# Filling all four weight slots behind each projection of the first mixer, with its convolutions as steps of their own

## The chip, the core and the metric

The kernel runs on one core of a Trainium2 chip. The metric is the device time of one execution in microseconds (us), where less is better. TensorE is called PE in the profile, VectorE DVE, ScalarE ACT, GpSimd POOL and SyncE SP (its DMA queue SPq).

## The reference

Two blocks of two layers each run over one sequence of 256 tokens with a width of 1024, all in float32. The change is mostly about the mixer of the first block:

```python
h = rms_norm(x, norm1_g)
proj = h @ w_in
qkv = silu(causal_depthwise_conv(qkv, dn_conv_w))      # four taps
q, k = l2_normalize(q), l2_normalize(k)
beta, g = sigmoid(b_in), -exp(dn_a_log) * softplus(a_in + dn_dt_bias)
o_dn = chunk_gated_delta_rule(q, k, v, g, beta)        # needs the inverse of a unit triangular matrix
o_dn = rms(o_dn) * dn_norm_g * silu(z)
y = gate_b * causal_depthwise_conv(gate_c * hv, sc_conv_w)   # three taps
x = x + concatenate([o_dn, rms(y)]) @ w_out
x = x + (silu(h2 @ ffn_w_gate) * (h2 @ ffn_w_up)) @ ffn_w_down
```

The second block takes its norms' scale and shift from `mod = silu(c) @ mod_w[l] + mod_b[l]`. This is a product of one row with a matrix of 1024 x 9216 per layer. It doesn't depend on `x`, so the kernel works it out beside the feed-forward stages (FFN).

## The kernel before

**Products in three parts.** Every float32 weight is split into a rounded high part and the rest: `h @ w` is `h_hi w_hi + h_lo w_hi + h_hi w_lo`. The weights come as units of 128 x 1024. ACT writes the high part of a unit (`round_weights`, the instruction on L970) and DVE the low part (`low_weights`, L1282, which waits for ACT's). PE may start a unit once its low part is there (`s_lo_ready`). `w_hi` and `w_lo` have four slots each, so unit v can be rounded once unit v - 4 has been used.

**Loads.** Two units make a chunk of 1 MB. SP loads chunks in the order of the steps into `raw`, a ring of four (L466). The load of chunk c waits until chunk c - 4 is used up: until the low parts of both its units are made, or, where it is a "mod" chunk, until DVE has reduced it. Most mod chunks go into a ring of their own (`side`, six places, L457). Those numbered 40 to 47 go through `raw`, since the memory of `side` is in use then.

**One list of steps.** `FIRST` and `SECOND` write out the order of a layer's steps by hand, and each engine walks through the same list and does its share of each step. An engine runs its instructions strictly in this order: what stands first and waits holds up all behind it. At a step with products, ACT and DVE first see to it that the weights are made up to two units past the step's own (`round_weights(n["split"] + units + 2)`, and `low_weights` with the same limit); at a filler step (mod, coef, table) up to four units from the next one on.

**The first mixer.** Its projections are pairs of 128-column tiles. `lead` is the first product of a pair and `pair` the second, each of 24 matmuls. For pairs 0 to 5 (q, k, v) ACT scales and copies both tiles out of PSUM (L1104, L1106) and DVE then adds three taps of the convolution in six instructions (L1440), both at the step `pair`. `silu` is a tanh on ACT (L1109) and a product on DVE (L1448). Pairs 6 and 7 are z (a tanh on ACT, L1112, and a product on DVE, L1454), pairs 8 to 11 are the short convolution (a copy on ACT, L1114, then L1460 to L1468 on DVE). `nsum` squares a tensor on ACT (L979) and sums it on PE (L714): 1 for k, 0 for q. `decay` is a chain through PE, DVE (L1426 to L1429) and ACT (L1084 to L1094). `kk` and `kq` are the products of keys and queries. `lvt` and `lvx` (1 to 6) build the triangular inverse level by level, each on PE (L763 and L774), then ACT (L1147) or DVE (L1552, L1555; level 6 on L1570). `scan` (L819 and what follows) is the recurrence. Both layers have this mixer, with the same times relative to its start.

**The FFN.** 33 steps: four `gu` (two wide products each, gate and up), then down, gu, gu in turn (`ffn_order`). Steps 4, 7, 10, ... are `down`. After a `gu`, ACT copies its sums to `sq` (L1186), DVE adds the rest (L1589), ACT takes a tanh (L1006), DVE makes `hid` (L1312, L1313), ACT rounds it (L1000), and POOL makes its low part (L1807), which `down` needs. `behind_ffn` spreads a list of mod steps over an FFN, here 20, 22 and 26 of them over the FFNs of block 1 layer 0, block 1 layer 1, and the second one of block 2 layer 0. `behind_steps` with `RAW_MODS` puts the eight raw mods behind steps 2, 6, 10, ..., 30 of the first FFN of block 2 layer 0. Each mod is two reductions on DVE (L1401). `COEFS` are small operations for the second mixer, put behind the steps in `COEF_STEPS`.

Of the kernel before, what the change touches and what calls it, by code (L numbers as in the profile page):

```python
# [48 lines left out]
COEFS = [("coef", 0), ("coef", 1), ("coef", 2), ("coef", 3), ("coef", 4), ("table", 0), ("coef", 5), ("table", 1),  # L49
         ("coef", 6), ("kzero", 0), ("coef", 7), ("table", 2), ("coef", 8), ("table", 3), ("coef", 9), ("table", 4),  # L50
         ("bzero", 0), ("table", 5), ("table", 6), ("table", 7)]
RAW_MODS = {2 + 4 * k: k for k in range(8)}
COEF_STEPS = [k for k in range(3, 29) if k not in RAW_MODS]
BLK = T // 2


def ffn_order():

    out = [("gu", k) for k in range(4)]
    for j in range(FT // 2):  # L60
# [4 lines left out]


FIRST = (
    [("norm", 0), ("pair", 0), ("crow", 0), ("lead", 1), ("silu", 0), ("pair", 1), ("gates", 0), ("lead", 6),
     ("silu", 1), ("pair", 6), ("gsum", 0), ("lead", 2), ("pair", 2), ("lead", 3), ("decay", 0), ("silu", 2),
     ("pair", 3), ("lead", 8), ("silu", 3), ("pair", 8), ("lead", 9), ("nsum", 1), ("nroot", 1), ("pair", 9), ("kk", 0),  # L70
     ("kq", 0), ("lead", 4), ("pair", 4), ("lead", 5), ("silu", 4), ("lvt", 1), ("tokk", 0), ("pair", 5), ("lvx", 1),
     ("lead", 10), ("silu", 5), ("lvt", 2), ("nsum", 0), ("nroot", 0), ("lvx", 2),
     ("pair", 10), ("lvt", 3), ("lead", 11), ("lvx", 3), ("pair", 11), ("lead", 12), ("lvt", 4),
     ("pair", 12), ("lvx", 4), ("lead", 13), ("lvt", 5), ("pair", 13), ("lvx", 5), ("tokv", 0), ("lead", 7),
     ("nsum", 2), ("lvt", 6), ("nroot", 2), ("pair", 7), ("lvx", 6), ("nrow", 2), ("scan", 0),
     ("out", 0), ("nsum", 3), ("nroot", 3), ("out", 1), ("nrow", 3), ("out", 2), ("dsplit", 0)]
# [23 lines left out]
    + [s for k, step in enumerate(ffn_order()) for s in  # L100
       [step] + [("grow", 0)] * (k == 9) + [c for at, c in zip(COEF_STEPS, COEFS) if at == k]]
    + [("post", 0), ("pre", 1)] + MIXER
# [6 lines left out]
FFN_STEPS = len(ffn_order())  # L109


def behind_ffn(steps, which, mods):

    places = [k for k, s in enumerate(steps) if s[2] in ("gu", "down")][which * FFN_STEPS + 6:(which + 1) * FFN_STEPS - 4]
    out, done = [], 0
    for k, s in enumerate(steps):
        out.append(s)
        if k in places:
            upto = len(mods) * (places.index(k) + 1) // len(places)
            out += mods[done:upto]  # L120
            done = upto
    return out
# [17 lines left out]
def second_block(L):  # L140
    return [(2, L, kind, i) for kind, i in SECOND]
# [4 lines left out]
        [(1, LAYERS - 1, "final", 0)] + \  # L146
        behind_ffn(behind_steps(second_block(0), 0, MODS[1][4:12], RAW_MODS), 1, MODS[1][12:]) + second_block(1)
SIDE_OF = {m: k for k, m in enumerate([m for m in range(MODT) if not 40 <= m < 48])}
# [36 lines left out]
AT = {(B, L, kind, i): n for B, L, kind, i, n in NUMBERED}  # L185
# [20 lines left out]
def build(nc, w, x_in, const_in, p1_in, p2_in, bt_in, out):  # L206
    with ExitStack() as ctx:
# [31 lines left out]
        crow = sb("crow", [P, D])  # L239
# [189 lines left out]
        def evacuated(e, *step):  # L429

            p = AT[step]["pair"]
            e.wait_ge(banks[p % 2], p // 2 + 1)
# [518 lines left out]
        def _(act):  # L951
# [64 lines left out]
            for B, L, kind, i, n in NUMBERED:  # L1016
                bank = stream[n["pair"] % 2]
                units = units_of(B, kind, i)
# [76 lines left out]
                elif kind == "pair" and B == 1 and i < 6:  # L1095
# [6 lines left out]
                    for e in range(2):  # L1102
                        last_tap = (2 * i + e) * TAPS + TAPS - 1
                        f(yv[:, 2 * (i % 2) + e, :], bank[:, e, :], ACT.Copy,  # L1104
                          scale=p1_(L, "conv", last_tap, last_tap + 1))
                    f(rawp[:, i % 2, :, 3:3 + T], bank[:], ACT.Copy).then_inc(free, 1)  # L1106
                elif kind == "silu":
                    act.wait_ge(s_conv_done, 12 * L + 2 * (i + 1))
                    f(th[:, 2 * (i % 2):2 * (i % 2) + 2, :], yv[:, 2 * (i % 2):2 * (i % 2) + 2, :], ACT.Tanh,  # L1109
                      scale=0.5).then_inc(s_th_done, 1)  # L1110
                elif kind == "pair" and B == 1 and i < 8:
                    f(zs[:, 2 * (i - 6):2 * (i - 6) + 2, :], bank[:], ACT.Tanh, scale=0.5).then_inc(s_z_th, 1)  # L1112
                elif kind == "pair" and B == 1 and i < 12:
                    f(sc[:, i - 8, :], bank[:, 0, :], ACT.Copy).then_inc(s_c_done, 1)  # L1114
                elif kind == "nsum":
                    src = [qT, kT, sc, None][i]

                    def n_ready(j):
# [121 lines left out]
                elif kind == "score":  # L1240
# [3 lines left out]
                    for e, cols in enumerate((slice(0, T), slice(T, T + P))):  # L1244
                        k = 2 * i + e
# [20 lines left out]
        def _(dve):  # L1266
# [3 lines left out]
            def link(ins):  # L1270
                links[0] += 1
                ins.then_inc(s_dve_self, 1)
                dve.wait_ge(s_dve_self, links[0])
# [3 lines left out]
            def low_weights(limit):  # L1277

                while fed[0] < min(limit, TOTAL["split"]):
                    q = fed[0]  # L1280
                    dve.wait_ge(s_hi_ready, q + 1)
                    v.tensor_tensor(w_lo[:, q % SLOTS, :],  # L1282
                                    raw[:, chunk_of_unit[q] % RAWS, (q % 2) * UNIT:(q % 2 + 1) * UNIT],
                                    w_hi[:, q % SLOTS, :].bitcast(F32), ALU.subtract).then_inc(s_lo_ready, 1)
                    fed[0] += 1
# [38 lines left out]
            for B, L, kind, i, n in NUMBERED:  # L1324
                bank = stream[n["pair"] % 2]
                units = units_of(B, kind, i)
# [63 lines left out]
                elif kind == "mod":  # L1390
                    dve.wait_ge(s_crow_done, 2)
                    if n["mod"] in SIDE_OF:
                        k = SIDE_OF[n["mod"]]
# [30 lines left out]
                elif kind == "decay":  # L1424
# [2 lines left out]
                    dve.wait_ge(s_gc_sb, L + 1)  # L1427
                    v.tensor_tensor(sm["d"], sm["gc"][:, 8:16], sm["gc"][:, 0:8], ALU.subtract).then_inc(s_dd_done, 1)
                    v.tensor_scalar(sm["ngc"], sm["gc"][:, 0:8], -1.0, None, ALU.mult).then_inc(s_dd_done, 1)  # L1429
                elif kind == "pair" and B == 1 and i < 6:  # L1430
                    evacuated(dve, B, L, kind, i)
                    if L == 0 and i == 0:
                        dve.wait_ge(s_pads, 1)
                    for k in range(TAPS - 1):
                        for e in range(2):
                            tile = 2 * i + e
                            y = yv[:, 2 * (i % 2) + e, :]
                            src = rawp[:, i % 2, e, k:k + T]
                            tap = p1_(L, "conv", tile * TAPS + k, tile * TAPS + k + 1)
                            ins = v.scalar_tensor_tensor(y, src, tap, y, ALU.mult, ALU.add)  # L1440
                            if k == TAPS - 2:
                                ins.then_inc(s_conv_done, 1)
                            elif e == 1:
                                link(ins)
                elif kind == "silu":
                    dve.wait_ge(s_th_done, 6 * L + i + 1)
                    dst = (qT, kT, vT)[i // 2]
                    v.scalar_tensor_tensor(dst[:, 2 * (i % 2):2 * (i % 2) + 2, :], th[:, 2 * (i % 2):2 * (i % 2) + 2, :],  # L1448
                                           1.0, yv[:, 2 * (i % 2):2 * (i % 2) + 2, :], ALU.add, ALU.mult)\
                        .then_inc(s_silu_done, 1)  # L1450
                elif kind == "pair" and B == 1 and i < 8:
                    t = 2 * (i - 6)
                    dve.wait_ge(s_z_th, 2 * L + i - 5)
                    v.scalar_tensor_tensor(zs[:, t:t + 2, :], zs[:, t:t + 2, :], 1.0, bank[:], ALU.add, ALU.mult)\  # L1454
                        .then_inc(free, 1)
                elif kind == "pair" and B == 1 and i < 12:
                    t = i - 8
                    dve.wait_ge(s_c_done, 4 * L + t + 1)
                    dve.wait_ge(s_pads, L + 1)
# [2 lines left out]
                    for k in range(STAPS):  # L1462
# [3 lines left out]
                            link(v.tensor_scalar(sc[:, t, :], src, tap, None, ALU.mult))  # L1466
                        else:
                            link(v.scalar_tensor_tensor(sc[:, t, :], src, tap, sc[:, t, :], ALU.mult, ALU.add))  # L1468
                elif kind == "pair" and B == 1:
                    t = 2 * (i - 12)  # L1470
                    v.tensor_tensor(sc[:, t:t + 2, :], sc[:, t:t + 2, :], bank[:], ALU.mult).then_inc(free, 1)
                elif kind == "nsum" and i == 3:
# [221 lines left out]
                elif kind == "fwd":  # L1694
                    k = 4 * L + i
# [10 lines left out]
                elif kind == "rec":  # L1706
                    k = 4 * L + i
# [7 lines left out]
                elif kind == "back":  # L1715
                    k = 4 * L + i
# [259 lines left out]
```

## Time and profile before

| | |
|---|---|
| Median of 3 runs | 1954.5 us (1952.48 to 1957.59) |
| Time of the profiled execution | 1957.57 us |
| Its span | 1955.2 us |
| PE busy | 1849.3 us, 95% of the span |
| DVE busy | 1472.1 us, 75% |
| ACT busy | 1064.5 us, 54% |
| POOL busy | 202.4 us, 10% |
| DMA engines busy (mean share, three queues) | 52.8% |
| TensorE clock granted, mean | 0.976 of full speed |

Times in the timeline count from the start of the span. By the timeline the first mixer of layer 0 lies at about 21 to 183 us and that of layer 1 at 381 to 540 us. The FFN with raw mods lies at 743 to 942 us, and the one with 26 mod steps at 1154 to 1347 us.

### The profile page before, as it was taken

The numbers are of one execution on the slowest core, as the hardware profiler recorded it, in microseconds if no ns is written. First come the engines' busy times: TensorE is split into PE (matmuls) and PEld (weight loads), VectorE is DVE, ScalarE is ACT, GpSimd is POOL, SyncE is SP. The second block draws the span as 40 slices with busy tenths as digits, with TensorE's granted clock in tenths as the row PEclk, the third lists the DMA queues.
The fourth block names the chain that finished last, engine by engine and source line by source line (L and its number), as shares of the span: only waits on it lengthen the run. The fifth ranks groups of instructions, "written<-read, shape, count | busy, mean of one in ns | idle before, by whom it ended". The sixth has DMA issues, their size and how long they took to land.

```text
span 1955.2 us, 31506 instructions
## 1 busy us (share of the span) xinstructions
PE 1849.3 (95%) x12640; PEld 1627.5 (83%) x12640; DVE 1472.1 (75%) x2339; ACT 1064.5 (54%) x1739; POOL 202.4 (10%) x174
## 2 busy tenths in 40 slices
PE   6999999998999998999799989998999899989998
PEld 5887888788978887888699978877888799978887
DVE  4756799875578987888677768997777767776565
ACT  5645555664465456656534565446566744556554
POOL 0100111101011111111000001110111100001111
PEclk9989999998999999999899989998999999999999
DMA  5332898433369864555343449974545343344452
GB/s 219 121 111 107 324 346 331 156 135 110 111 264 357 319 220 162 215 216 215 131 150 130 158 179 359 362 301 160 194 173 193 130 152 122 119 170 167 178 194 86
DMA packets 53280, 383.50 MB, mean 196 GB/s; under 512 B 5904, under 2 KB 6032, under 8 KB 6928
## 3 DMA queue, kind: packets, MB, share of 16 engines
q1 hardware_dynamic: 53136, 381.50, 52.4%
q8 instruction: 100, 1.64, 0.3%
q14 instruction: 44, 0.36, 0.1%
HBM read 380.43 MB, written 1.05 MB: 195 GB/s over the span
## 4 chain that ended last, share of the span: by engine, by line
PE 74%; DVE 13%; ACT 7%; issue 4%; DMA 2%; POOL 0%; SPq 0%; DVEq 0%; ACTq 0%
PE quad L505 20%; PE quad L506 10%; PE quad L495 6%; PE quad L496 5%; PE quad L497 5%; PE works L517 4%; PE works L519 4%; PE works L518 4%; ACT w_hi L970 3%; DVE w_lo L1282 3%; DMA raw<-w 2%; DVE mx L1401 2%; DVE mx L1440 1%; PE works L676 1%; PE works L888 1%
## 5 line engine op out<-in xcount | busy, mean ns | idle before, releaser
L1282 DVE TENSOR_TENSOR w_lo<-raw,w_hi 128x1024 fp32r<-128x1024 f32 x572 | 700.5, 1233 | 211.5 <-ACT w_hi L970 209.9
L505 PE MATMUL quad<-h_two,w_hi 128*128 128x512 f32 x2112 | 755.9, 401 | 14.5 <-DVE h_two L1290 9.7
L970 ACT ACTIVATE w_hi<-raw 128x1024 fp32r<-128x1024 f32 x572 | 595.8, 1054 | 213.6 <-PE quad L506 95.2
L506 PE MATMUL quad<-h_two,w_lo 128*128 128x256 f32 x2112 | 596.2, 282 | 0.0
L505 PEld LDWEIGHTS quad<-h_two,w_hi 128*128 128x128 f32 x2112 | 401.1, 190 | 116.5 <-issue 18.7
L506 PEld LDWEIGHTS quad<-h_two,w_lo 128*128 128x128 f32 x2112 | 403.1, 191 | 2.0
L1807 POOL TENSOR_TENSOR g_lo<-hid,g_hi 128x256 fp32r<-128x256 f32 x140 | 177.5, 1269 | 1516.4 <-ACT g_hi L1000 1516.4
L495 PE MATMUL quad<-h_two,w_hi 128*128 128x256 f32 x960 | 280.3, 292 | 10.7 <-DVE w_lo L1282 10.7
L496 PE MATMUL quad<-h_two,w_hi 128*128 128x256 f32 x960 | 274.2, 286 | 0.0
L497 PE MATMUL quad<-h_two,w_lo 128*128 128x256 f32 x960 | 273.7, 285 | 0.0
L495 PEld LDWEIGHTS quad<-h_two,w_hi 128*128 128x128 f32 x960 | 186.3, 194 | 15.6 <-issue 13.9
L517 PE MATMUL works<-w_hi,g_hi 128*128 128x512 f32 x480 | 189.2, 394 | 0.4 <-DVE w_lo L1282 0.4
L519 PE MATMUL works<-w_lo,g_hi 128*128 128x512 f32 x480 | 187.7, 391 | 0.0
L518 PE MATMUL works<-w_hi,g_lo 128*128 128x512 f32 x480 | 187.2, 390 | 0.0
L496 PEld LDWEIGHTS quad<-h_two,w_hi 128*128 128x128 f32 x960 | 186.6, 194 | 0.0
L497 PEld LDWEIGHTS quad<-h_two,w_lo 128*128 128x128 f32 x960 | 186.4, 194 | 0.0
L1401 DVE CUSTOM_DVE_ANT_0 mx<-mx,crow 128x1024 f32<-128x1024 f32 x128 | 151.0, 1217 | 0.0
L1000 ACT ACTIVATE g_hi<-hid 128x256 fp32r<-128x256 f32 x140 | 57.4, 412 | 149.3 <-DVE hid L1313 145.6
L1186 ACT ACTIVATE sq<-quad 128x512 f32<-128x512 f32 x132 | 78.0, 591 | 99.8 <-PE quad L506 99.3
L1589 DVE TENSOR_TENSOR sq<-sq,quad 128x512 f32<-128x512 f32 x132 | 90.2, 683 | 53.8 <-ACT sq L1186 53.2
L519 PEld LDWEIGHTS works<-w_lo,g_hi 128*128 128x128 f32 x480 | 90.1, 188 | 20.3
L517 PEld LDWEIGHTS works<-w_hi,g_hi 128*128 128x128 f32 x480 | 90.1, 188 | 19.9 <-issue 0.7
(408 smaller groups left out, 2184.2 us busy)
## 6 DMA issues: line engine op xcount, KB each, us to landing
raw<-w SPq DMA_DIRECT2D x294, 1024.0 KB, 4.9
mx<-w SPq DMA_DIRECT2D x64, 1024.0 KB, 7.0
par<-p_in SPq DMA_DIRECT2D x2, 1110.0 KB, 7.1
x<-x_in SPq DMA_DIRECT2D x1, 1024.0 KB, 5.6
mx<-bt_in SPq DMA_DIRECT2D x2, 512.0 KB, 6.0
out<-x SPq DMA_DIRECT2D x4, 256.0 KB, 2.3
con<-const_in SPq DMA_DIRECT2D x1, 428.0 KB, 3.0
par<-p_in SPq DMA_DIRECT2D x1, 225.0 KB, 5.7
```

Source lines behind the costliest of these rows:

```text
L495: mm(o, hi, r_hi[:, kt, :], start=first, stop=False, skip_group_check=True)
L496: mm(o, hi, r_lo[:, kt, :], start=False, stop=False, skip_group_check=True)
L497: last = mm(o, lo, r_hi[:, kt, :], start=False, stop=end, skip_group_check=True)
L505: mm(o, hi, h_two[:, kt, :, :], start=kt == 0, stop=False, skip_group_check=True)
L506: return mm(o[:, 0:T], lo, h_hi[:, kt, :], start=False, stop=kt == DT - 1, skip_group_check=True)
L517: mm(sums[q][:], a_hi, hi, start=first, stop=False)
L518: mm(sums[q][:], a_lo, hi, start=False, stop=False)
L519: last = mm(sums[q][:], a_hi, lo, start=False, stop=end)
L970: f(w_hi[:, v % SLOTS, :], raw[:, chunk_of_unit[v] % RAWS, (v % 2) * UNIT:(v % 2 + 1) * UNIT], ACT.Copy).then_inc(s_hi_ready, 1)
L1282: v.tensor_tensor(w_lo[:, q % SLOTS, :], raw[:, chunk_of_unit[q] % RAWS, (q % 2) * UNIT:(q % 2 + 1) * UNIT], w_hi[:, q % SLOTS, :].bitcast ...
L1401: v.tensor_tensor_reduce(rows, rows, crow[:], 1.0, 0.0, ALU.mult, ALU.add, modacc[:, 2 * i + e:2 * i + e + 1]).then_inc(s_mod_used, 1)
L1807: v.tensor_tensor(g_lo[:, slot, :], hid[:, g % 2, :], g_hi[:, slot, :].bitcast(F32), ALU.subtract)\
```

## The change

- `pair` 0 to 5 is split: ACT's copies stay at `pair`, and DVE's part becomes a step `conv`, placed by hand. At `conv` DVE waits for ACT's copies, does the six instructions, and then makes low parts up to four units past the pair's own. For pair 1 it stands behind `gates`, for 0, 2, 3 and 4 behind the next `lead`, and for 5 behind `lvx` 2.
- At the end of `pair` 0 to 11, ACT rounds weights up to four units past the pair's own; DVE does the same with the low parts at the end of `pair` 6 to 11.
- `nsq` 0, the squares of q on ACT, stands behind `kq`. PE's sum and `nroot` 0 stay where `nsum` 0 is.
- `silu` 5 moves from behind `lead` 10 to behind `pair` 10.
- The raw mods stand behind steps 2, 4, 6, 10, 14, 18, 22 and 26. `coef` 0 and 1 move from behind steps 3 and 4 to behind 1 and 3 (in both layers); the others stay.
- `behind_ffn` starts one step earlier, at 5, and spreads over 24 places in place of 23.

```diff
-RAW_MODS = {2 + 4 * k: k for k in range(8)}
-COEF_STEPS = [k for k in range(3, 29) if k not in RAW_MODS]
+RAW_MODS = {at: k for k, at in enumerate((2, 4, 6, 10, 14, 18, 22, 26))}
+COEF_STEPS = [1] + [k for k in range(3, 29) if k not in RAW_MODS]
 FIRST = (
-    [("norm", 0), ("pair", 0), ("crow", 0), ("lead", 1), ("silu", 0), ("pair", 1), ("gates", 0), ("lead", 6),
-     ("silu", 1), ("pair", 6), ("gsum", 0), ("lead", 2), ("pair", 2), ("lead", 3), ("decay", 0), ("silu", 2),
-     ("pair", 3), ("lead", 8), ("silu", 3), ("pair", 8), ("lead", 9), ("nsum", 1), ("nroot", 1), ("pair", 9), ("kk", 0),
-     ("kq", 0), ("lead", 4), ("pair", 4), ("lead", 5), ("silu", 4), ("lvt", 1), ("tokk", 0), ("pair", 5), ("lvx", 1),
-     ("lead", 10), ("silu", 5), ("lvt", 2), ("nsum", 0), ("nroot", 0), ("lvx", 2),
-     ("pair", 10), ("lvt", 3), ("lead", 11), ("lvx", 3), ("pair", 11), ("lead", 12), ("lvt", 4),
+    [("norm", 0), ("pair", 0), ("crow", 0), ("lead", 1), ("conv", 0), ("silu", 0), ("pair", 1), ("gates", 0),
+     ("conv", 1), ("lead", 6), ("silu", 1), ("pair", 6), ("gsum", 0), ("lead", 2), ("pair", 2), ("lead", 3), ("conv", 2),
+     ("decay", 0), ("silu", 2), ("pair", 3), ("lead", 8), ("conv", 3), ("silu", 3), ("pair", 8), ("lead", 9), ("nsum", 1),
+     ("nroot", 1), ("pair", 9), ("kk", 0), ("kq", 0), ("nsq", 0), ("lead", 4), ("pair", 4), ("lead", 5), ("conv", 4),
+     ("silu", 4), ("lvt", 1), ("tokk", 0), ("pair", 5), ("lvx", 1),
+     ("lead", 10), ("lvt", 2), ("nsum", 0), ("nroot", 0), ("lvx", 2), ("conv", 5),
+     ("pair", 10), ("silu", 5), ("lvt", 3), ("lead", 11), ("lvx", 3), ("pair", 11), ("lead", 12), ("lvt", 4),
      ("pair", 12), ("lvx", 4), ("lead", 13), ("lvt", 5), ("pair", 13), ("lvx", 5), ("tokv", 0), ("lead", 7),
      ("nsum", 2), ("lvt", 6), ("nroot", 2), ("pair", 7), ("lvx", 6), ("nrow", 2), ("scan", 0),
...
 def behind_ffn(steps, which, mods):
-    places = [...][which * FFN_STEPS + 6:(which + 1) * FFN_STEPS - 4]
+    places = [...][which * FFN_STEPS + 5:(which + 1) * FFN_STEPS - 4]
...
 ACT, kind == "pair" and B == 1 and i < 6:
                     f(rawp[:, i % 2, :, 3:3 + T], bank[:], ACT.Copy).then_inc(free, 1)
+                    round_weights(n["split"] + units + 4)
 ACT, kind == "pair" and B == 1 and i < 8 (and the same at i < 12):
                     f(zs[:, 2 * (i - 6):2 * (i - 6) + 2, :], bank[:], ACT.Tanh, scale=0.5).then_inc(s_z_th, 1)
+                    round_weights(n["split"] + units + 4)
 ACT:
-                elif kind == "nsum":
+                elif kind in ("nsum", "nsq") and (kind, i) != ("nsum", 0):
 DVE:
-                elif kind == "pair" and B == 1 and i < 6:
-                    evacuated(dve, B, L, kind, i)
+                elif kind == "conv":
+                    evacuated(dve, 1, L, "pair", i)
...
+                    low_weights(AT[1, L, "pair", i]["split"] + units_of(1, "pair", i) + 4)
 DVE, at the end of pair 6, 7 and of pair 8 to 11:
+                    low_weights(n["split"] + units + 4)
```

## Rows read from the trace of the kernel before

**Rows 1.** The page: each engine's busy time.

```profile
PE 1849.3 (95%) x12640; PEld 1627.5 (83%) x12640; DVE 1472.1 (75%) x2339; ACT 1064.5 (54%) x1739; POOL 202.4 (10%) x174
```

**Rows 2.** Busy time by stretch: us, PE, PEld, DVE, ACT, POOL, clock, DMA, GB/s.

```profile
380.00:457.00 77.00, 67.71 (x680) 65.66 (x680) 57.67 (x112) 50.22 (x96) 9.21 (x9) 1.00 0.33 116
461.00:469.00 8.00, 8.00 (x135) 7.82 (x136) 2.01 (x4) 0.22 (x1) 0.00 (x0) 0.56 0.26 86
740.00:941.00 201.00, 192.35 (x1060) 162.77 (x1059) 164.95 (x248) 122.19 (x179) 28.22 (x22) 0.98 0.53 214
```

**Rows 3.** Waits of PE, 380 to 540 us: total us, times, longest.

```profile
PE quad L495 <- DVE w_lo L1282: 5.4, 5, 1.3
PE works L763 <- DVE mx L1552: 3.1, 1, 3.1
```

**Rows 4.** Timeline of ACT at pair 3 (layer 1).

```profile
419.25 0.83 ACT L1104 ACTIVATE mx<-quad,par 128x256 f32<-128x256 f32 x2
...
420.45 1.07 ACT L970 ACTIVATE w_hi<-raw 128x1024 fp32r<-128x1024 f32 x1
...
426.12 1.14 ACT L979 ACTIVATE sq<-mx 128x512 f32<-128x512 f32 x2
```

**Rows 5.** Timeline of DVE at pair 3 (layer 1).

```profile
420.67 2.71 DVE L1440 SCALAR_TENSOR_TENSOR mx<-mx,par 128x256 f32<-128x256 f32 x6
423.31 1.22 DVE L1282 TENSOR_TENSOR w_lo<-raw,w_hi 128x1024 fp32r<-128x1024 f32 x1
```

**Rows 6.** Timeline of PE, 427 to 464 us.

```profile
427.61 1.84 PE L714 MATMUL quad<-con,sq 128*128 128x1 f32 x16
...
457.33 0.83 PE L763 MATMUL works<-mx 32*32 32x32 f32 x64 [3.10 <-DVE mx L1552]
459.24 3.54 PE L714 MATMUL quad<-con,sq 128*128 128x1 f32 x16 [1.08 <-ACT sq L979]
...
463.69 0.58 PE L495 MATMUL quad<-h_two,w_hi 128*128 128x256 f32 x1
```

**Rows 7.** Timeline of DVE, then of PE, ahead of the scan (layer 1).

```profile
503.62 0.69 DVE L1454 SCALAR_TENSOR_TENSOR mx<-mx,quad 128x512 f32<-128x512 f32 x1 [1.19 <-ACT mx L1112]
504.23 0.74 DVE L1570 TENSOR_SCALAR mx<-works 64x256 f32<-64x256 f32 x2
...
505.77 1.06 PE L819 MATMUL works<-mx 128*128 128x128 f32 x8
```

**Rows 8.** Loads of raw, 745 to 800 us: all issues on L466.

```profile
DMA to landing us min/median/max: 4.8/6.9/10.3
```

**Rows 9.** Timelines of ACT, DVE and PE, 762 to 783 us.

```profile
770.22 1.06 ACT L970 ACTIVATE w_hi<-raw 128x1024 fp32r<-128x1024 f32 x1 [1.80 <-DMA raw<-w]
...
765.25 0.08 DVE L1401 DVE_READ_ACCUMULATOR2_ANT modacc<- 128x1 f32 x1
...
771.19 0.39 PE L505 MATMUL quad<-h_two,w_hi 128*128 128x512 f32 x1
```

**Rows 10.** DVE and PE at the end of the FFN, layer 0, then layer 1.

```profile
928.74 1.22 DVE L1401 CUSTOM_DVE_ANT_0 raw<-raw,crow 128x1024 f32<-128x1024 f32 x1
...
931.03 0.42 DVE L1312 SCALAR_TENSOR_TENSOR gate_t<-gate_t,sq 128x256 f32<-128x256 f32 x1
...
933.68 0.80 PE L535 MATMUL works<-w_hi,g_hi 128*128 128x512 f32 x1 [4.99 <-POOL g_lo L1807]
...
1542.50 0.50 PE L535 MATMUL works<-w_hi,g_hi 128*128 128x512 f32 x1 [0.34 <-POOL g_lo L1807]
```

**Rows 11.** DVE, then PE, behind step 21 of the FFN with 26 mods.

```profile
1287.44 1.22 DVE L1401 CUSTOM_DVE_ANT_0 mx<-mx,crow 128x1024 f32<-128x1024 f32 x1
...
1292.03 0.42 DVE L1312 SCALAR_TENSOR_TENSOR gate_t<-gate_t,sq 128x256 f32<-128x256 f32 x1
...
1294.19 0.77 PE L505 MATMUL quad<-h_two,w_hi 128*128 128x512 f32 x1 [2.64 <-DVE w_lo L1282]
1294.96 0.63 PE L505 MATMUL quad<-h_two,w_hi 128*128 128x512 f32 x1
```

More of the change, by code:

```diff
@@ L112, in behind_ffn @@
 def behind_ffn(steps, which, mods):
-    places = [k for k, s in enumerate(steps) if s[2] in ("gu", "down")][which * FFN_STEPS + 6:(which + 1) * FFN_STEPS - 4]
+    places = [k for k, s in enumerate(steps) if s[2] in ("gu", "down")][which * FFN_STEPS + 5:(which + 1) * FFN_STEPS - 4]
     out, done = [], 0
@@ L1112, in _ @@
                     f(zs[:, 2 * (i - 6):2 * (i - 6) + 2, :], bank[:], ACT.Tanh, scale=0.5).then_inc(s_z_th, 1)
+                    round_weights(n["split"] + units + 4)
                 elif kind == "pair" and B == 1 and i < 12:
                     f(sc[:, i - 8, :], bank[:, 0, :], ACT.Copy).then_inc(s_c_done, 1)
-                elif kind == "nsum":
+                    round_weights(n["split"] + units + 4)
+                elif kind in ("nsum", "nsq") and (kind, i) != ("nsum", 0):
                     src = [qT, kT, sc, None][i]
@@ L1450, in _ @@
                         .then_inc(s_silu_done, 1)
-                elif kind == "pair" and B == 1 and i < 8:
+                elif kind == "pair" and B == 1 and 6 <= i < 8:
                     t = 2 * (i - 6)
@@ L1455, in _ @@
                         .then_inc(free, 1)
-                elif kind == "pair" and B == 1 and i < 12:
+                    low_weights(n["split"] + units + 4)
+                elif kind == "pair" and B == 1 and 8 <= i < 12:
                     t = i - 8
@@ L1468, in _ @@
                             link(v.scalar_tensor_tensor(sc[:, t, :], src, tap, sc[:, t, :], ALU.mult, ALU.add))
-                elif kind == "pair" and B == 1:
+                    low_weights(n["split"] + units + 4)
+                elif kind == "pair" and B == 1 and i >= 12:
                     t = 2 * (i - 12)
```

## The prediction

> **What bounds the kernel.** I read the busy table first: PE is busy 95% of the span [rows 1], so only PE's pauses, and stretches at a lower clock, can be won. The stretches by stage come second. In the first mixer's earlier half PE is busy 67.7 of 77 us at full clock, while no other engine is full and DMA stands at 0.33; in the FFN with the raw mods it misses about 9 of 201 us [rows 2]. Third come PE's waits in the mixer: five waits for low parts of weights, 5.4 us; 3.1 us of `lvt` 2 for `lvx` 1's update on DVE [rows 3]; 1.08 us of `nsum` 0 for the squares of q shows in the timeline [rows 6]. Last, the timelines around each pause show what the late instruction stood behind. Both layers have the same mixer, so each figure for it counts twice.
>
> **Mixer, what is removed.** The five waits are worth 5.4 us [rows 3]. `lvx` 1 no longer stands behind convolution 5, and the squares of q are made early: the 3.10 and 1.08 us in front of `lvt` 2 and `nsum` 0 go [rows 6]. With them goes a stretch at the lower clock: the stretch from 461 us has a mean of 0.56 [rows 2], so between 1.2 and 2.4 GHz. PE was idle most of the 5 us before. It costs `nsum` 3.54 against 1.84 us elsewhere, 1.7 us [rows 6], and I put the product behind it at 2.0 us (its 24 matmuls of about 0.12 us each start over 24 x 0.12 = 2.9 us at full clock). In all 5.4 + 4.2 + 3.7 = 13.3 us per mixer.
>
> **Mixer, what is added.** The fill adds no instruction; it moves roundings ahead of other work on two engines that run in order. Four places matter.
>
> (a) At `lead` 3, 8 and 5 DVE's low part now stands ahead of the convolution, and waits for ACT's high part, which waits for ACT's copies. Before, convolution 3 started 1.42 us behind the start of the copies [rows 4, 5]. Now it is copies 1.33, rounding 1.0, low part 1.14: 3.5 us behind. ACT reaches the copies of pair 3 no earlier than before, since the chain of `decay` on ACT ends there: convolution 2, late by the same mechanism, starts `decay` some 0.9 us later, and one rounding of 0.95 us that stood behind it is gone. So the low part for `lead` 9 comes at about 422.8 (before 423.31 + 1.22 = 424.5), and PE waits there 3.3 us instead of 0.8, having been earlier by then.
>
> (b) Convolution 3 ends 2.1 us later, and the two roundings filled behind `pair` 8 (now 2.0 us, of which one stood there before) precede the squares of k. These start at 428.4 in place of 426.12 [rows 4], so `nsum` 1 starts at 429.1 in place of 427.61 [rows 6], after a second pause of about 3.2 us. PE is then 1.5 us later than before; the fifth wait's 1.2 us comes back behind it. The five weight waits are thus spent on two larger ones: net +0.2 us.
>
> (c) ACT's copies for `lvt` 1 and `lvt` 2 stand behind convolution 4's tanh and behind two filled roundings: `lvx` 1 and 2 wait 1.0 and 1.3 us. Net of the 13.3 us, PE reaches product `pair` 10 at about 459.6 in place of 463.69 [rows 6], and gains 2.0 more in it: 6.1 us.
>
> (d) Behind `pair` 7, DVE now makes two low parts (2.4 us) ahead of L1570, on which the scan waits. In the trace L1570 runs at 504.23 to 504.97, right behind L1454, and PE starts the scan at 505.77 with no pause [rows 7]. Now it ends at 507.5: +2.0 us. The scan's chain has no slack to return it.
>
> Without clock effects this is 6.1 - 2.0 = 4.1 us per mixer. But two pauses of over 3 us within 10 us of each other, with `nsum` behind the second, look like those that cost the clock at 461 us. A pause of only 2.64 us was enough in an FFN: its next matmuls are 0.63 us apart, against 0.35 later [rows 11]. I charge one slow stretch, `nsum` 1.7 and most of a product 1.6: 3.3 us. Ends: none, or twice that (a second one at `lvx` 2). Two mixers give -2 x (4.1 - 3.3) = **-1.6 us**.
>
> The Trainium skill, "TensorE: Matmul & The Clock Gate", section "Why this matters for your kernels", says that a long idle gap between bursts of matmuls sets the clock back; the 2.64 us row is shorter than the gap that it warns of, so the trace is harsher than the rule. If (a) and (b) were harmless as the rule would have it, the mixers would give -8.2 us.
>
> **FFN with raw mods, its end.** The mod behind step 30 goes. Its 2.3 us stand straight ahead of L1312, and through `hid`, ACT and POOL ahead of the last `down`, where PE waits 4.99 us; layer 1, without mods, waits 0.34 [rows 10]. I take 2.3 us; what is left is about 2.7 us of pause. The first matmul behind it takes 0.80 us instead of 0.50 [rows 10]: PE is at the lower clock there. If 2.7 us spares the clock, 2.5 us more.
>
> **FFN with raw mods, its start.** A mod behind step 4 takes a place in the ring of four. Chunk order becomes mod 0, gu 3, down 0, mod 1, gu 4. So gu 4's load, before the fourth behind nothing but gu 2, now waits until mod 0 is reduced, at 765.3 [rows 9]. A load takes 4.8 us at the least [rows 8] (gu 5's, which stood there before, landed in time for the rounding at 770.22 [rows 9]). Rounding 1.05 and low part 1.2 put gu 4 at 772.65 in place of 771.19 [rows 9]: +1.5. Worse, ACT and DVE stand still for it from 763 on. Behind it come, in order, the sum of gu 3 (773.2), a low part, coef 1, `hid` (775.9), two low parts (778.6), and only then mod 1, until 781.0. Down 1's load waits for that: landed at 785.8, low part ready at 788.1. PE is done with gu 5 at 772.65 + 4 x 2.83 = 784.0, and pauses 4.3 us. Together 5.8 us. The clock falls in it as it does at 933.68, so that charge moves rather than goes (2.5 us on both sides). Later mods stand where they stood, about 3 us more behind PE, which the 12 us between mod and need still covers. 5.8 - 2.3 = **+3.5 us**. Ends: -4.8 (the loads are in time) and +10 (down 2's load, which waits for mod 2, is late too).
>
> **The FFN with 26 mod steps.** By the formula, before there were two mods behind steps 13 and 21; now one more stands at 5 and the double is at 16. Both lists are at 9 behind step 13, 18 behind 21, and 24 behind 27. From step 13 on DVE has no free time (in the timeline its pauses are 0.2 to 0.3 us), and behind step 21 its 4.6 us of reductions make PE wait 2.64 us [rows 11]. Up to step 12 the new list has done 8 against 7, in DVE's free time: one reduction, 2.37 us, leaves the full stretch. **-2.4 us**; ends 0 and -4.2 (pause and slow matmuls both).
>
> **No cost.** The FFNs with 20 and 22 mods show no pause of PE over 0.34 us, and get no double: 0. The coef operations moved by a step are 12 of 0.2 us beside a full PE: 0.
>
> **Sum.** -1.6 + 3.5 - 2.4 = -0.5 us on the profiled span of 1955.2, the same on its own time of 1957.57; that execution is 3 us above the median, so I count from the median: 1954.5 - 0.5 = **1954.0 us**.
>
> **Rivals.**
> 1. The clock holds in the mixers, or the two new pauses are shorter than I count. For: they are split by a dense product. Against: the row of 2.64 us. -8.2 there, +3.5 - 2.5 = +1.0 and -2.4: -9.6, 1944.9. Chance 0.20.
> 2. Down 1's load comes in time, because DVE gets to mod 1 within 6 us rather than 15. The FFN gives -4.8 instead of +3.5: 1954.0 - 8.3 = 1945.7. Against: the ring's order leaves gu 4 no earlier load. Chance 0.10.
> 3. Slower: the raw ring stays late. Each mod is reduced late, the next load with it, and PE pauses at down 2 as at down 1: 4.3 and 2.5 of clock, +6.8: 1960.8. It decides if mod 2 ends later than 7 us ahead of down 2's start; I count 7.2 us, so it is near. Chance 0.23.
> 4. The fill does nothing: slots are free no earlier than the old order asked, and only `lvt` 2 gains and the scan pays. The time would still be 1952 to 1956. Chance 0.05.
>
> My forecast has 0.42. About 0.3% (5.9 us) is what a measurement of this kernel can tell from no change. Rivals 1 and 2 are faster by more (0.30), the forecast and rival 4 lie within (0.47), and rival 3 is slower (0.23). The range takes rivals 1 and 3 in: 1944 to 1963. The forecast alone, with its bounds, is 1949 to 1959.
>
> **What would show it.** PE's five waits for L1282 in the mixer gone; a pause of about 3 us ahead of `lead` 9 and one ahead of `nsum` 1, in both layers; `lvt` 2 without a pause; the scan starting behind L1570, with two low parts ahead of it. PE pausing about 4 us before down 1 of the FFN with raw mods, on DMA through ACT and DVE, and about 2.7 us at its end. No 2.64 us pause in the FFN with 26 mods. I am wrong if convolution 3 starts as early as before, or if down 1 starts without a pause.

## The result and the profile after

The changed kernel takes 1960.91 us (median of 15 runs, 1954.99 to 1965.86), against 1954.92 us (15 runs, 1949.06 to 1957.59) for the kernel before beside it: a ratio of 1.0029, 95% interval 1.0019 to 1.0038, so 5.7 us more (3.7 to 7.4). One further execution of the kernel before, beside e5 to e8, took 4619.77 us and, as the only slow one, is left out of every ratio. I had said 1954.0 us. The time lies inside my range, but it moved the way to which I gave 0.23. The profiled execution took 1963.98 us, its span is 1961.9 us.

Busy time of each engine, from the page of the changed kernel:

```profile
PE 1855.1 (95%) x12640; PEld 1631.8 (83%) x12640; DVE 1470.0 (75%) x2339; ACT 1065.7 (54%) x1739; POOL 199.7 (10%) x174
```

The counts are those of before [rows 1], and PE is busy 5.8 us longer with the same 12640 matmuls. The mean granted clock is 0.973, before 0.976, and 0.003 of 1960 us is 5.9 us. PE is idle for 106.8 us (the span less the busy time), before 105.9: of the 6.7 us between the two spans 0.9 us are pauses, and the rest is time at the lower clock.

Between the first transposition of one norm and that of the next, the timelines give this (us, before and after): mixer of layer 0 167.5 and 167.6, its FFN 193.7 and 193.6; mixer of layer 1 163.7 and 161.8, its FFN 197.1 and 201.1; FFN with raw mods 208.0 and 216.9; FFN with 26 mods 203.2 and 201.0. So one profile puts the loss into the raw FFN and into an FFN that the change touches only in the places of some of its mod steps, and shows the mixers no slower. The timed experiments will say something else about the edit of the mixers.

**The mixer of layer 1.** Waits of PE, 375 to 540 us, changed kernel: what was waited for, total us, times, longest.

```profile
PE works L820 <- DVE mx L1577: 2.7, 1, 2.7
PE quad L496 <- DVE w_lo L1286: 2.5, 1, 2.5
...
PE works L775 <- ACT mx L1151: 2.3, 3, 0.8
...
PE quad L715 <- ACT sq L980: 1.5, 1, 1.5
```

The five weight waits and the 3.1 us of `lvt` 2 [rows 3] are gone, as the change meant. In their place stand one weight wait ahead of `lead` 9, one for the squares of k, three short ones at `lvx` 1 to 3, and one ahead of the scan. Together 9.0 us against 9.6.

Timelines of ACT, then DVE, then PE at pair 3 (start, us, what, [idle before <- releaser]):

```profile
418.26 0.83 ACT L1105 ACTIVATE mx<-quad,par 128x256 f32<-128x256 f32 x2
...
419.45 2.01 ACT L971 ACTIVATE w_hi<-raw 128x1024 fp32r<-128x1024 f32 x2
...
425.31 1.99 ACT L971 ACTIVATE w_hi<-raw 128x1024 fp32r<-128x1024 f32 x2
427.20 1.14 ACT L980 ACTIVATE sq<-mx 128x512 f32<-128x512 f32 x2
...
420.62 1.23 DVE L1286 TENSOR_TENSOR w_lo<-raw,w_hi 128x1024 fp32r<-128x1024 f32 x1 [1.35 <-ACT w_hi L971]
421.77 2.71 DVE L1444 SCALAR_TENSOR_TENSOR mx<-mx,par 128x256 f32<-128x256 f32 x6
...
422.00 0.36 PE L496 MATMUL quad<-h_two,w_hi 128*128 128x256 f32 x1 [2.50 <-DVE w_lo L1286]
...
427.87 1.95 PE L715 MATMUL quad<-con,sq 128*128 128x1 f32 x16 [1.47 <-ACT sq L980]
```

This is the order that I had described: copies, rounding, low part, and only then the convolution, 3.5 us behind the start of the copies (1.42 before [rows 4, 5]). Both pauses are smaller than I had: 2.5 in place of 3.3 and 1.5 in place of 3.2 us.

**Ahead of the scan.** Timelines of ACT, DVE and PE, changed kernel:

```profile
496.00 1.28 ACT L1114 ACT_TABLE_LOAD   x1
497.29 0.60 ACT L1114 ACTIVATE mx<-quad 128x512 f32<-128x512 f32 x1
497.79 1.99 ACT L971 ACTIVATE w_hi<-raw 128x1024 fp32r<-128x1024 f32 x2
...
498.00 0.69 DVE L1459 SCALAR_TENSOR_TENSOR mx<-mx,quad 128x512 f32<-128x512 f32 x1 [0.76 <-ACT mx L1114]
498.87 2.36 DVE L1286 TENSOR_TENSOR w_lo<-raw,w_hi 128x1024 fp32r<-128x1024 f32 x2 [0.18 <-ACT w_hi L971]
501.15 0.74 DVE L1577 TENSOR_SCALAR mx<-works 64x256 f32<-64x256 f32 x2
...
501.94 2.08 PE L820 MATMUL works<-mx 128*128 128x128 f32 x8 [2.70 <-DVE mx L1577]
503.81 1.74 PE L824 MATMUL works<-mx 128*128 128x128 f32 x8
505.39 1.06 PE L828 MATMUL works<-mx 128*128 128x128 f32 x8
```

The two low parts stand ahead of L1577 (L1570 of before), which ran right behind L1454 then [rows 7]. The pause is 2.70 us, and behind it the first two groups of the scan take 2.08 and 1.74 us in place of the 1.06 us of the third [rows 7]: PE is at the lower of its two levels, 1.2 GHz. I had charged the pause at 2.0 us and no clock. Whether these slow groups are a cost that the fill adds, e5 will show.

**The FFN with raw mods.** ACT and PE, changed kernel:

```profile
774.87 1.06 ACT L971 ACTIVATE w_hi<-raw 128x1024 fp32r<-128x1024 f32 x1 [8.14 <-DMA raw<-w]
...
790.27 1.06 ACT L971 ACTIVATE w_hi<-raw 128x1024 fp32r<-128x1024 f32 x1 [8.54 <-DMA raw<-w]
...
777.33 0.47 PE L506 MATMUL quad<-h_two,w_hi 128*128 128x512 f32 x1 [1.41 <-DVE w_lo L1286]
...
792.73 0.77 PE L518 MATMUL works<-w_hi,g_hi 128*128 128x512 f32 x1 [4.06 <-DVE w_lo L1286]
...
945.21 0.51 PE L536 MATMUL works<-w_hi,g_hi 128*128 128x512 f32 x1 [2.71 <-POOL g_lo L1814]
```

All three pauses are where and about as long as forecast (1.5, 4.3 and 2.7 us). ACT stands still for 8 us twice, for the two loads. No pause follows at `down` 2, which rules rival 3 out, although its time came nearest.

**The FFN with 26 mods.** PE:

```profile
1338.59 0.47 PE L506 MATMUL quad<-h_two,w_hi 128*128 128x512 f32 x1 [1.76 <-DVE w_lo L1286]
```

The 2.64 us pause of [rows 11] is gone; a later one is 1.76 us, where 0.75 stood. The stage is 2.2 us shorter.

### The profile page after: what moved, and what is told of

Read it like the earlier page. It is cut to its first block, busy times and chain, and to the rows that moved or that the text cites. A ratio compares the mean times of both kernels' runs of the same rounds, so it can differ in the third digit from the quotient of the medians.

```text
span 1961.9 us, 31505 instructions
## 1 busy us (share of the span) xinstructions
PE 1855.1 (95%) x12640; PEld 1631.8 (83%) x12640; DVE 1470.0 (75%) x2339; ACT 1065.7 (54%) x1739; POOL 199.7 (10%) x174
## 4 chain that ended last, share of the span: by engine, by line
PE 72%; DVE 12%; ACT 9%; issue 4%; DMA 2%; POOL 0%; SPq 0%; DVEq 0%; ACTq 0%
PE quad L506 20%; PE quad L507 10%; PE quad L496 5%; PE quad L497 5%; PE quad L498 5%; PE works L518 4%; PE works L520 4%; PE works L519 4%; ACT w_hi L971 4%; DVE w_lo L1286 3%; DMA raw<-w 2%; DVE mx L1405 2%; PE works L677 1%; DVE mx L1444 1%; PE works L889 1%
```

## The experiments

Each ratio is to the kernel before on the same chip; its medians were 1955.28, 1955.22 and 1955.23 us in the three sets. The column "us" is the ratio less 1, times 1955. The last one is the granted clock, the mean over the executions of the run; it is 0.9773, 0.9772 and 0.9777 for the kernel before in the three sets, and 0.9755 for the changed kernel. e5 and e8 rest on 5 executions, e12 on 6, e7 on 11, the others on 12.

| run | what | median us | ratio (95%) | us | clock |
|---|---|---|---|---|---|
| e1_raw_only | raw mods and coef steps | 1958.71 | 1.0020 (1.0005 to 1.0034) | +3.9 | 0.9787 |
| e2_places_only | `behind_ffn` | 1952.74 | 0.9988 (0.9977 to 1.0000) | -2.3 | 0.9782 |
| e3_mixer_only | whole mixer change | 1958.16 | 1.0023 (1.0008 to 1.0038) | +4.5 | 0.9737 |
| e4_order_only | order of steps, no fill | 1949.65 | 0.9982 (0.9965 to 0.9998) | -3.5 | 0.9794 |
| e5_no_fill_pair7 | e3 less the fill behind pair 7 | 1949.32 | 0.9962 (0.9949 to 0.9975) | -7.4 | 0.9774 |
| e6_conv_first | e3, convolutions 0 to 4 at once | 1952.86 | 0.9982 (0.9966 to 0.9998) | -3.5 | 0.9766 |
| e7_raw_even | raw mods at 0, 4, ..., 28 | 1952.38 | 0.9983 (0.9971 to 0.9995) | -3.3 | 0.9778 |
| e8_together | e4, e2 and e7 | 1943.22 | 0.9936 (0.9924 to 0.9948) | -12.5 | 0.9804 |
| e9_after_no_fill_pair7 | the change less the fill behind pair 7 | 1952.85 | 0.9991 (0.9977 to 1.0006) | -1.8 | 0.9767 |
| e10_fill_pair7_only | before plus the fill behind pair 7 | 1960.36 | 1.0026 (1.0016 to 1.0035) | +5.1 | 0.9768 |
| e11_fill_pair7_act_only | e3, DVE's low parts of that fill left out | 1953.03 | 0.9984 (0.9971 to 0.9996) | -3.1 | 0.9758 |
| e12_all_but_pair7 | all that helped | 1939.09 | 0.9913 (0.9896 to 0.9930) | -17.0 | 0.9803 |

### The parts alone

e1: the first two lines of the diff, on the kernel before.

> The kernel before with the raw mods behind steps 2, 4, 6, 10, 14, 18, 22 and 26 and coef 0 and 1 behind 1 and 3, nothing else. Theory A (the loss is in this FFN): the pauses of the changed kernel's trace stay, 1.4 us ahead of gu 4 and 4.1 us ahead of down 1, with one stretch of slow clock behind them that the old order had at the FFN's end; slower by 4 to 8 us. Theory B (the loss is the clock at the norms, whose place the mixer moved): this part costs the 3.5 us of the prediction or less, and the rest of the 5.7 us is not here.

e2: its `behind_ffn` line.

> The kernel before with behind_ffn from step 5 over 24 places, nothing else. Both theories: the pause of 2.64 us behind step 21 of the FFN with 26 mod steps shrinks to about 0.3 us, a pause near the end grows from 0.75 to about 1.8 us; faster by about 2.2 us.

e3: all of the mixer's lines (`FIRST`, `conv`, `nsq`, the fill).

> The kernel before with the changed order of the first mixer, the convolutions as steps, the squares of q ahead and the fill; raw mods, coef and places as before. Theory A: the mixers' own time falls by 0 to 2 us each, as in the changed kernel's trace, and the whole is faster by 1 to 3 us. Theory B: the mixers move the norms against the clock, and the whole is 1 to 5 us slower although the mixers themselves are no longer.

The parts are +3.9, -2.3 and +4.5 us, and their sum of 6.1 us is the whole's 5.7. The FFNs came out as predicted (+3.5 and -2.4); the edit of the mixers, which I had at -1.6, costs 4.5 us (1.6 to 7.4). So the loss that I did not see comes with this edit, though the profile of the whole change shows the mixers no slower.

Against what was expected: e1 lies between its two theories and its interval (1.0 to 6.6) separates neither, and its trace has the three pauses (1.44, 3.96 and 2.73 us). e2 came out as expected. In e3 theory A (1 to 3 us faster) fell, and the time lies in the range of theory B, a loss by the clock. The clocks on record bear this out: 0.9737 in e3 against 0.9773. A straight line through the clocks and times of the 35 executions of the kernel before gives 1.0 us for each 0.001 of clock, and one through e3's 12 gives 1.2. So the lower clock alone would cost e3 3.7 to 4.3 us (an estimate), about its whole loss, while its pauses are no longer than before.

e4: the order alone. Convolutions 0 to 4 stand right behind their pairs, as before, and nothing is filled.

```diff
-     ("lead", 10), ("silu", 5), ("lvt", 2), ("nsum", 0), ("nroot", 0), ("lvx", 2),
-     ("pair", 10), ("lvt", 3), ...
+     ("lead", 10), ("lvt", 2), ("nsum", 0), ("nroot", 0), ("lvx", 2), ("conv", 5),
+     ("pair", 10), ("silu", 5), ("lvt", 3), ...
+    ("nsq", 0) behind ("kq", 0)
```

> The kernel before with two parts of the mixer's change alone: the squares of q behind kq, and convolution 5 behind lvx 2 (silu 5 behind pair 10). Convolutions 0 to 4 stand right behind their pairs, as before, and nothing is filled. The five waits for weights (5.4 us) stay; the pauses ahead of lvt 2 and nsum 0 (4.2 us) and the slow stretch behind them (3.7 us) go, in both mixers; no pause ahead of nsum 1, and none for two low parts ahead of the scan. If the fill gives back what it wins (theory A), this is 8 to 14 us faster than the kernel before. If the fill is what wins in the mixers, it is no faster than the kernel with the whole mixer change.

Waits of PE in the mixer of layer 1, e4:

```profile
PE quad L496 <- DVE w_lo L1283: 5.4, 5, 1.3
...
PE works L764 <- DVE mx L1553: 0.3, 1, 0.3
```

Its granted clock (the third number from the end) at `lvx` 2 and the product behind it, then the same place in the changed kernel:

```profile
453.00:461.00 8.00, 6.06 (x86) 5.78 (x76) 4.39 (x9) 0.19 (x1) 0.00 (x0) 0.57 0.15 47
```

```profile
455.00:463.00 8.00, 7.39 (x224) 6.97 (x224) 4.57 (x11) 4.12 (x10) 0.00 (x0) 1.00 0.17 67
```

The five weight waits are all there, the wait of `lvt` 2 is 0.3 us in place of 3.1, and the kernel is 3.5 us faster than before (0.4 to 6.8). I had expected 8 to 14: that missed. A pause of 1.94 us, for which the trace names no releaser, now stands inside `lvx` 2, and the slow stretch behind it, which I had expected to go, is there in e4. In the changed kernel it is gone. Beside e3, the fill with the later convolutions takes 5.4 us of weight waits out of each mixer, and still leaves the kernel 4.5 + 3.5 = 8.0 us slower than this one.

### Which part of the fill

e5: no fill behind pair 7.

```diff
-                    round_weights(n["split"] + units + 4)
+                    if i == 6:
+                        round_weights(n["split"] + units + 4)
```

and the same for `low_weights` on DVE.

> The whole mixer change (as in e3_mixer_only, 1958.2 us), but without the fill behind pair 7. Theory A (roundings filled ahead of work that PE waits for cost the mixers their gain): the pause of 2.7 us ahead of the scan goes in both layers, and the two low parts come back behind the scan's first product, where nothing waits: about 5 us less than e3_mixer_only, 1953 us. Theory B (the pauses are harmless, and e3_mixer_only was slow because the clock fell at the norms of the FFN behind): the time stays within 1.5 us of 1958, and FFN 1 of layer 1 stays 2.5 us or more longer than the 197.1 us of the kernel before.

It is 8.8 us faster than e3 by the medians (7.4 + 4.5 = 11.9 by the ratios), more than the 5 us that I had reckoned for the pauses alone. Timelines of DVE and PE ahead of its scan:

```profile
496.04 0.69 DVE L1460 SCALAR_TENSOR_TENSOR mx<-mx,quad 128x512 f32<-128x512 f32 x1 [1.01 <-ACT mx L1114]
496.65 0.74 DVE L1579 TENSOR_SCALAR mx<-works 64x256 f32<-64x256 f32 x2
...
498.19 1.06 PE L820 MATMUL works<-mx 128*128 128x128 f32 x8
499.08 1.06 PE L824 MATMUL works<-mx 128*128 128x128 f32 x8
```

No pause, and 1.06 us for each of the groups that took 2.08 and 1.74. It is tempting to add up 2.7 us of pause and 1.02 + 0.68 = 1.7 us of slow groups per layer to 2 x 4.4 = 8.8 us, as I did before e9. That sum is not shown. Here are the 37 us that end just behind the scan's first groups, in the changed kernel, in e5 and in the kernel before:

```profile
470.00:507.00 37.00, 34.30 (x464) 33.15 (x463) 20.37 (x37) 16.57 (x25) 3.11 (x6) 0.95 0.38 140
```

```profile
466.00:503.00 37.00, 37.00 (x489) 35.94 (x488) 19.03 (x37) 15.06 (x23) 3.12 (x6) 0.95 0.32 116
```

```profile
474.00:511.00 37.00, 37.00 (x489) 35.99 (x488) 19.77 (x37) 15.46 (x24) 3.12 (x6) 0.95 0.32 115
```

The granted clock is 0.95 in all three. Without the fill the slow stretch lies in the product ahead of the scan, and in the changed kernel in the scan: it moved and did not grow. And in e3's own layer 0 the pause is 1.63 us, with full-speed groups behind it. So the pauses of e3 come to 1.63 + 2.69 = 4.3 us, half or less of what e5 wins. The rest goes with the clock of the whole execution, 0.9774 for 0.9737; no one place of it was found (e3's trace has 169.3 us for the mixer of layer 0 and 161.8 for that of layer 1, e5's 162.0 and 164.0).

Theory B held that nothing here matters but the clock at the norm of the FFN behind. That FFN stayed long in e5 (199.5 us against 197.1) while the time fell, so the clock at that norm can't be what made e3 slow. The clock elsewhere can.

e9: the same lines taken out of the whole change.

> The changed kernel without the fill behind pair 7, everything else as in the change. Theory A, in its present form (the two low parts ahead of L1577 cost each layer 2.7 us of pause ahead of the scan and 1.7 us in which the scan's first two products run at the lower clock): 2 x 4.4 = 8.8 us less than the changed kernel's 1960.9: 1952.1 us, a ratio of 0.9985. Rival (the gain from dropping the fill in the kernel with the mixer change alone came from where the clock fell elsewhere): 1957 us or more.

1952.85 us, where 1952.1 were expected, and 7.4 us less than the changed kernel by the ratios: this one fill turns the whole change from 5.7 us slower into one that can't be told from the kernel before. The 8.8 us behind that expectation were made up wrongly, so the agreement in size is in part chance. The mixer of layer 1, in the changed kernel and in e9:

```profile
376.60:538.40 161.80, 148.87 (x1657) 140.69 (x1657) 104.32 (x196) 87.27 (x158) 11.62 (x15) 0.97 0.33 118
```

```profile
373.50:533.70 160.20, 150.13 (x1656) 142.02 (x1657) 104.62 (x196) 87.25 (x158) 11.64 (x15) 0.96 0.34 119
```

PE's idle time falls from 12.9 to 10.1 us, which is the pause, and its busy time rises by 1.3 us, since here the clock is lower.

e10: only this fill added to the kernel before.

```diff
+                    if i == 7:
+                        round_weights(n["split"] + units + 4)
...
+                    if i == 7:
+                        low_weights(n["split"] + units + 4)
```

> The kernel before with one part of the change: the fill behind pair 7. Theory A: a pause of 2 to 3 us ahead of the scan in both layers, and the scan's first products slow behind it: 7 to 9 us more than before, 1962 to 1964 us, a ratio of 1.004. Rival (the pause comes from filling every slot before, which makes four slots fall due at once; alone, the fill finds its slots in use or filled): within 2 us of 1955.

5.1 us slower (3.1 to 6.8), where I expected 7 to 9: the direction is right, the size too large. PE ahead of its scan:

```profile
507.17 1.16 PE L819 MATMUL works<-mx 128*128 128x128 f32 x8 [1.63 <-DVE mx L1574]
508.17 1.06 PE L823 MATMUL works<-mx 128*128 128x128 f32 x8
```

Here the pause is 1.63 us in both layers, 3.3 of the 5.1 us, and the clock holds. The difference to 2.70 is ACT. In e10, as in the kernel before, ACT's tanh waits for PE; in the changed kernel PE's product is done while ACT still loads its table (496.00 to 497.28 above), so ACT, and DVE behind it, are later against PE. In e10 the product runs at the lower clock just there, and that gives ACT its time. (In e3's layer 0, where the pause is 1.63 us too, the product also runs at the lower clock.) The rival (alone, the fill does nothing) fell.

e11: e3, where ACT rounds early behind pair 7 and DVE doesn't.

> The whole mixer change, where behind pair 7 ACT rounds up to four units ahead but DVE makes no low parts early. Theory A (the low parts on DVE stand ahead of L1577): no pause ahead of the scan, 1949 to 1951 us, as without either. Rival (ACT's two roundings of 1.05 us ahead of its copies are what is late): a pause of 1.5 us or more stays ahead of the scan or behind its second product, 1955 us or more.

PE's wait ahead of the scan is 0.2 us:

```profile
PE works L820 <- DVE mx L1578: 0.2, 1, 0.2
```

DVE's low parts are therefore what PE waits for. The time, 1953.0, is 5.1 us under e3 (7.6 by the ratios) and 3.7 over e5, and two over what I expected. The intervals of e5 and e11 overlap, so whether ACT's early roundings cost something by themselves stays open.

### The order at pair 3

e6: e3 with the convolutions 0 to 4 right behind their pairs, as in e4's `FIRST`.

> The whole mixer change, but the convolutions 0 to 4 stand right behind their pairs, as before, so that the low parts for the next lead stand behind the convolution; the fill is kept. Theory A: convolution 3 no longer waits for ACT's rounding, PE's pauses ahead of lead 9 (2.5 us) and of nsum 1 (1.3 us) shrink to 1 us each at most, and the time is 4 to 5 us below e3_mixer_only, 1953 to 1954 us. Rival: ACT's roundings filled behind the pairs are what makes convolution and squares late, not DVE's order; then both pauses stay within 0.5 us of what they were, and the time is 1957 to 1959 us.

The time is the one of theory A, the pauses are not. Waits of PE in the mixer of layer 1:

```profile
PE quad L496 <- DVE w_lo L1286: 3.1, 1, 3.1
PE works L820 <- DVE mx L1577: 2.7, 1, 2.7
PE works L692 <- ACT gate_t L1073: 1.5, 1, 1.5
PE works L775 <- ACT mx L1151: 0.8, 1, 0.8
```

The pause ahead of `lead` 9 grew from 2.5 to 3.1 us, since the low part now stands behind the convolution; the one at `nsum` 1 and those at `lvx` 1 and 2 went, and one at `gsum` came. In sum 8.1 against e3's 9.2 us, and 5.3 us of time (8.0 by the ratios). The clock is 0.9766 against e3's 0.9737, which by the slopes above is some 3 us of it (an estimate). Neither order starts `lead` 9 on time.

### The raw mods

e7: four steps apart everywhere, each two steps earlier than before.

```diff
-RAW_MODS = {2 + 4 * k: k for k in range(8)}
-COEF_STEPS = [k for k in range(3, 29) if k not in RAW_MODS]
+RAW_MODS = {4 * k: k for k in range(8)}
+COEF_STEPS = [1, 2, 3, 5, 6, 7, 9, 10, 13, 15, 17, 18, 19, 21, 22, 23, 24, 25, 26, 27]
```

> The kernel before with the raw mods behind steps 0, 4, 8, ..., 28: the last mod two steps earlier as in the change, but four steps apart everywhere; eight coefficient steps move by one or two places. Theory A (mods two steps apart at the start are what costs the FFN its 5.5 us, since a ring of four makes the load of gu 4 and of down 1 wait for a reduction that waits itself): no pause over 1 us ahead of gu 4 or down 1, the pause at the end 2.7 us in place of 5.0: 2.3 us less than before, 1953 us (clock aside). Rival (any early mod makes the ring late, since DVE must finish it before the load three chunks on): a pause of 2 us or more ahead of gu 4 or down 1 stays, and the time is 1956 to 1959 us.

Waits of PE in its raw FFN:

```profile
PE works L535 <- POOL g_lo L1807: 4.0, 1, 4.0
PE quad L505 <- DVE w_lo L1282: 0.9, 1, 0.9
```

Nothing waits ahead of `gu` 4 or `down` 1. So it is two mods two steps apart, in a ring of four, that cost the change its 5.5 us there; an early mod as such does not. The end won only 1.0 us of pause (5.0 to 4.0) where I had expected 2.3; in the change, with the last mod at 26 and not 28, 2.7 us are left. The time is 3.3 us under before (1.0 to 5.7).

### What beats both

e8: e4's order, e2 and e7.

> Only the parts that helped: convolution 5 and silu 5 later, the squares of q early, no fill, behind_ffn over 24 places, raw mods behind 0, 4, ..., 28. If the parts add (before 1955.3; order -5.6, places -2.4, raw mods -2.3): 1945 us, a ratio of 0.995. If a part won only by where the clock happened to stand in it: 1949 us or more.

e12: e8 with the fill everywhere but behind pair 7.

> Everything that helped, together: convolutions 0 to 4 right behind their pairs, the fill everywhere but behind pair 7, convolution 5, silu 5 and the squares of q moved, behind_ffn over 24 places, raw mods behind 0, 4, ..., 28. If the parts add (before 1955.2; fill and order without pair 7 -5.9, convolutions first -5.3, places -2.4, raw mods -2.9): 1938.7 us, a ratio of 0.9916. If the fill is worth nothing beyond the order of the steps: 1943 us, as without any fill. If the pause of 3.1 to 3.6 us that this order has ahead of lead 9 costs the clock: 1946 us or more.

Both came out as sums: 1943.2 us where 1945 were expected, and 1939.1 where 1938.7 were. The waits of PE in the mixer of layer 1 of e12:

```profile
PE quad L496 <- DVE w_lo L1287: 3.6, 1, 3.6
PE works L677 <- DVE mx L1350: 1.9, 1, 1.9
PE works L692 <- ACT gate_t L1073: 1.5, 1, 1.5
...
```

Ahead of the scan nothing is left (the 1.9 us belong to the norm behind). e12 is 0.87% faster than the kernel before (0.70 to 1.04%) and 21.8 us under the changed kernel. The fill seems worth some 4 us of it (e12 against e8, though their intervals overlap), and its price is the pause ahead of `lead` 9. That pause of 3.6 us did not cost e12 the clock: it is 0.9803, e8's 0.9804.

## Why the prediction was wrong

- **Five weight waits, `lvt` 2, squares of q.** Right: all gone, and `lvt` 2 starts without a pause (e4 too shows 0.3 for 3.1 us). The slow stretch behind them is gone too (clock 1.00 from 455 to 463 us).
- **(a), (b).** Right in place and mechanism, too large: 2.5 and 1.5 us for 3.3 and 3.2. The clock fell behind them, as charged (stretch 421 to 432 below), but the sums of `nsum` 1, charged at 1.7 us, took 1.95 us for 1.84.
- **(c).** 0.8, 0.6 and 0.8 us at three `lvx` steps for 1.0 and 1.3 at two: right in sum. My addition here doesn't close: 4.2 + 1.7 - 0.2 - 2.3 is 3.4 us up to `pair` 10, and I wrote 4.1. With 3.4 the mixers would have been -0.2 and not -1.6 us. PE did reach `pair` 10 at 459.50, where I had 459.6.
- **(d), the step that failed, with the clock term beside it.** I put the fill behind pair 7 at +2.0 us per mixer and no clock. The pause is 2.70 us where the product ahead runs at full clock, and 1.63 where it runs slow; I took mine from a trace of the second kind. Taking the fill out of the change wins 7.4 us by the ratios (e9), and out of e3 8.8 by the medians (e5), in place of my 4.0: 3.7 to 4.4 us per mixer for 2.0. Pauses are 5.4 us of e9's 7.4 and 4.3 of e5's 8.8. What is left goes with a lower clock over the execution (0.9737 with the fill for 0.9774 in e3 and e5; 0.9755 for 0.9767 in the change and e9, too little to be sure of), at no place that I could find, and its cause stays open; the slow groups of the scan aren't it, for as long a slow stretch stands ahead of the scan without the fill.
- **The clock in the mixers.** I gave 3.7 us per mixer back and charged 3.3, so that the edit would have left the clock a little better. The sum of the pauses came out right (9.0 for 9.6 us in layer 1; my terms without the clock give 0.4 less), and the clock did not: 0.9737 in e3 for 0.9773, some 4 us. With 8.8 for 4.0 in (d) the mixers become -1.6 + 4.8 = +3.2 us (measured +4.5, 1.6 to 7.4) and the whole +4.3 us (measured +5.7, 3.7 to 7.4). Without this fill my terms gave -5.6 us for the mixers; e5 has -7.4 (-10.0 to -4.9).
- **Raw FFN.** Right: +3.5, measured +3.9 (1.0 to 6.6), with the three pauses as described.
- **26 mods.** Right: -2.4, measured -2.3 (-4.5 to 0.0).
- **Rivals.** Rival 1 (the clock holds) fell: it fell at three places in each mixer. Rival 2 fell at the 4.06 us pause. Rival 3's mechanism did not occur; its 1960.8 us agrees with the result by chance. None of the rivals made the scan the loser, though (d) named it.

The granted clock, by stretch (us, PE, PEld, DVE, ACT, POOL, clock, DMA, GB/s), changed kernel at pair 3 and at the norm behind the mixer:

```profile
421.00:432.00 11.00, 8.54 (x53) 8.28 (x53) 9.77 (x19) 4.30 (x7) 0.00 (x0) 0.76 0.37 109
536.00:552.00 16.00, 12.02 (x52) 9.80 (x51) 9.70 (x23) 8.04 (x21) 0.00 (x0) 0.68 0.17 58
```

## What to carry to other kernels

Work made ahead of need is free only behind everything that another engine waits for: on an engine that runs in order, two early weight parts of 1.2 us each ahead of one small operation on the path cost PE a pause of up to 2.7 us in each layer and the change 7.4 us in all, when the whole fill was there to save 5.4 us of waits in each layer. Look for the places where the filled engine hands something to the bounding one, and leave these unfilled, one by one. When the change makes the bounding engine earlier, price each new wait in the new order of arrival, not in the old trace. Before you put a slow stretch down to the pause ahead of it, look for the same stretch in the kernel without the pause. And compare the granted clocks of all executions, not of the profiled one alone: here they showed a loss that no single trace did.

## What the runs showed that I had not expected

Pauses of about the same length were followed by either clock. The Trainium skill, "TensorE: Matmul & The Clock Gate", section "Why this matters for your kernels", warns of longer gaps than the 2.64 us behind which the kernel before has slow matmuls [rows 11]. In that row this case is harsher. But e1, which doesn't edit that FFN, has the same pause there without them:

```profile
1295.81 0.47 PE L505 MATMUL quad<-h_two,w_hi 128*128 128x512 f32 x1 [2.64 <-DVE w_lo L1282]
```

```profile
1295.00:1299.00 4.00, 3.19 (x18) 2.83 (x19) 3.71 (x5) 3.31 (x4) 1.20 (x1) 1.00 1.00 414
```

The clock is 1.00 there, and in the kernel before, where that first matmul takes 0.77 us, the clock is 0.57 from 1294 to 1298 us. So the row on which I rested the charge for short pauses shows what can happen, not what must. The norm behind the mixer of layer 1 has the same three pauses of PE in each kernel, 1.9, 0.5 and 1.6 us by the timelines, and different clocks. First the kernel before, then e5, 16 us from just ahead of it:

```profile
539.00:555.00 16.00, 12.30 (x74) 10.60 (x75) 12.64 (x27) 12.49 (x26) 0.00 (x0) 1.00 0.22 84
```

```profile
532.00:548.00 16.00, 12.88 (x64) 11.00 (x64) 10.60 (x23) 10.64 (x24) 0.00 (x0) 0.79 0.18 63
```

Full clock in the first, and in e4 too; 0.79 in e5, and 0.68 in the changed kernel above. With that the FFN behind it is 2.4 us longer in e5, which doesn't edit that FFN, and 4.0 us longer in the changed kernel, where PE is busy 192.7 us in it for 188.7. So an edit of one stage can cost time in the next, and a stage's time in one profile can mislead: the timed runs put 4.5 us on the mixers' edit, and the profile of the changed kernel puts none into the mixers and 4.0 us there. What decides the clock at this norm was not found.
